# A hybrid convolution, sparse-attention and feed-forward block on one core: merged rows kept in PSUM, x loaded first, woven products and count turns moved

## The reference

```
h  = rmsnorm(x); u = h @ w_in               # [conv a,gate 1024 | q 512 | k,v 64+64 | index q 512 | index k 64 | w 8 | gates 2048]
yc = silu(layernorm(causal_depthwise_conv31(a * sigmoid(gate)))) @ w_conv_out
score[t,s] = sum_heads w[t] * relu(qi[t] . ki[s]),  s <= t;   keep the 256 best keys s of each row t
ya = softmax(q.k/8 - slope*(t-s) over the kept keys) @ v, 8 heads;   ya @ w_attn_out
x1 = x + (sigmoid(gA) * yc + sigmoid(gB) * ya) @ w_out
x2 = x1 + (silu(rmsnorm(x1) @ w_gate) * (rmsnorm(x1) @ w_up)) @ w_down      # inner width 2816
out = rmsnorm(x2)
```

## Time and profile before

| | |
|---|---|
| median of 3 runs | 3352.51 us (3343.8 to 3353.59) |
| the profiled execution | 3356.66 us, span 3354.5 us, mean granted clock 0.981 |
| PE busy | 3200.5 us, 95% of the span |
| DVE, ACT, POOL busy | 2065.4, 1310.3, 743.8 us (62, 39, 22%) |
| chain that ended last | PE 75%, DVE 7%, ACT 4%, issue 4%, DMA 1% |
| DMA | 635.97 MB, mean 190 GB/s |

### The profile page before, as it was taken

The page is one execution under the profiler, slowest core; times in us unless marked ns, Lnnn a source line. Parts: engine busy times, 40 slices in busy tenths (PEclk is TensorE's granted clock), DMA queues, the critical chain, the costliest instruction groups (busy, mean ns, idle before and its releaser), DMA issues.

```text
span 3354.5 us, 41929 instructions
## 1 busy us (share of the span) xinstructions
PE 3200.5 (95%) x15077; PEld 2640.3 (79%) x15077; DVE 2065.4 (62%) x3529; ACT 1310.3 (39%) x2277; POOL 743.8 (22%) x546
## 2 busy tenths in 40 slices
PE   8987999999999999999999999999899998989998
PEld 7865788788888788778887778876788887778886
DVE  5997457688808448598994853759868288610001
ACT  4336421533238431441113843137773177421111
POOL 3431200065774000011322400000211323001212
PEclk9998999999999999999999999999999999999999
DMA  7973756599992656535554055652455510445554
GB/s 228 304 239 122 290 191 207 182 288 291 289 297 108 245 202 218 182 145 195 190 199 145 20 220 203 219 199 81 163 191 198 195 51 20 171 150 193 196 189 169
DMA packets 178528, 635.97 MB, mean 190 GB/s; under 512 B 11357, under 2 KB 96905, under 8 KB 116776
## 3 DMA queue, kind: packets, MB, share of 16 engines
q1 hardware_dynamic: 163728, 582.00, 50.2%
q10 hardware_dynamic: 14616, 51.47, 3.9%
HBM read 474.04 MB, written 159.38 MB: 189 GB/s over the span
## 4 chain that ended last, share of the span: by engine, by line
PE 75%; DVE 7%; ACT 4%; issue 4%; DMA 1%; POOL 0%; ACTq 0%; DVEq 0%; POOLq 0%; SPq 0%
PE PS L1763 19%; PE PS L1725 14%; PE PS L1727 14%; PE PS L1726 14%; PE PS L1930 3%; PE PS L1748 1%; PE PS L1749 1%; PE PS L1750 1%; DVE probs L1593 1%; PE PS L1949 1%; PE PS L1950 1%; PE PS L1809 1%; ACT TMP L838 1%; ACT probs L958 1%; PE PS L1977 1%
## 5 line engine op out<-in xcount | busy, mean ns | idle before, releaser
L1763 PE MATMUL PS<-WS,HT 128*128 128x512 f32 x2088 | 484.3, 392 | 16.1 <-ACT TMP L1082 10.4
L1763 PEld LDWEIGHTS PS<-WS,HT 128*128 128x128 f32 x2088 | 394.5, 189 | 99.7 <-ACT TMP L1082 10.8
L553 POOL TENSOR_TENSOR WS<-RAW,WS 128x1024 fp32r<-128x1024 f32 x116 | 281.1, 2424 | 577.5 <-ACT WS L709 562.2
L1725 PE MATMUL PS<-HF,WS 128*128 128x512 f32 x1024 | 400.5, 391 | 6.9 <-DVE HF L1171 4.6
L637 POOL TENSOR_TENSOR TMP<-TMP 128x512 f32<-128x512 f32 x88 | 113.6, 1291 | 1316.2 <-ACT TMP L1082 1316.2
L1726 PE MATMUL PS<-HF,WS 128*128 128x512 f32 x1024 | 400.1, 391 | 0.0
L1727 PE MATMUL PS<-HF,WS 128*128 128x512 f32 x1024 | 400.0, 391 | 0.0
L1351 DVE TENSOR_SCALAR_CACHE_REDUCE flags<-W,cand 128x640 uint8<-128x640 f32 (+9 forms) x272 | 372.6, 1370 | 35.6 <-DVE cand L1386 27.8
L1725 PE MATMUL PS<-HT,WS 128*128 128x512 f32 x816 | 322.2, 395 | 0.8 <-POOL WS L553 0.6
L1727 PE MATMUL PS<-HT,WS 128*128 128x512 f32 x816 | 317.7, 389 | 0.0
L1726 PE MATMUL PS<-HT,WS 128*128 128x512 f32 x816 | 317.6, 389 | 0.0
(11 more groups left out here) (283 smaller groups left out, 6490.0 us busy)
## 6 DMA issues: line engine op xcount, KB each, us to landing
WS<-split_weights_scratch SPq DMA_DIRECT2D x234, 1024.0 KB, 4.8
split_weights_scratch<-WS SPq DMA_DIRECT2D x116, 1024.0 KB, 5.0
W<-split_weights_scratch SPq DMA_DIRECT2D x114, 1024.0 KB, 4.8
RAW<-in_w_in SPq DMA_DIRECT2D x34, 512.0 KB, 6.0
RAW<-in_w_ffn_gate SPq DMA_DIRECT2D x22, 512.0 KB, 6.3
RAW<-in_w_ffn_up SPq DMA_DIRECT2D x22, 512.0 KB, 6.4
RAW<-in_w_ffn_down SPq DMA_DIRECT2D x22, 512.0 KB, 5.7
gate_b_scratch<-TMP ACTq DMA_DIRECT2D x32, 256.0 KB, 5.3
```

The costliest lines, as they stand in the source:

```text
L553: nc.gpsimd.tensor_tensor(out=WS[:, slot, 1, :], in0=RAW[:, slot, :], in1=WS[:, slot, 0, :].bitcast(f32), op=ALU.subtract).then_inc(w_lo, 1)
L1725: mm(PS[:, bank, :], wh, src[:, 0, k, :], start=k == 0, stop=False)
L1763: ins = mm(PS[:, 2 * t + half, :], lhs, split(c, w_part)[:, half * 512:(half + 1) * 512], start=first and part == 0 and w_part == 0, stop= ...
```

## The change

Nine edits, in the order of the program:

1. **Start.** SP loads all four row tiles of x before anything else (ACT loaded tiles 2 and 3 behind the small vectors). The transposes of the small vectors (`vectors()`, formerly L1772 and L1774, which wait for the seven small loads) move from PE's first place to behind 12 of the 16 scaled-identity products.
2. **Half chunks.** The first half of a half chunk raises a semaphore of its own, `first_half_psum`; DVE's product with the gate waits for that half (L1529 in A, L1639 in C) and no longer for the whole chunk.
3. **Merge in PSUM.** Product and sum of the merge are written in place in banks 0 to 7; ACT and DVE read them there. PE's half chunks no longer wait for `mg_sum`; w_out's first row chunk goes over row tiles 0 to 3 in order, each waiting for the eighths that free its two banks.
4. **POOL in C0.** `lo(c0 + 1)` waits for `at_ready`, so it starts after DVE's low parts of the attention output.
5. **Woven steps.** The 48 matmuls are spread anew: 6 at unit 4, 10 in the last unit, the other 32 evenly between. (Before: evenly over units 4 to last.)
6. **F2.** ACT's count turn behind the gate copy of pair j is done only for j % 4 = 3 (before: for every j not divisible by 4). The turn behind the up copy stays.
7. **C3.** The last two row chunks of w_out are joined row tile by row tile (`last_row_chunks`): each tile's twelve matmuls of both chunks stand together.
8. **C3.** ACT leaves out its waits for PE's chunk counts beside w_out in the last group, which stood ahead of the sum of squares (L731).
9. **F3.** The first gate chunk goes to bank 0 (`pair_bank`) and waits for `t_ready` eighth by eighth, not for all eight.

The diff, its core:

```diff
@@ -123,2 +123 @@
-late = 4
-return range(2 * 3 * KD * max(0, n - late) // (IDX_UNITS[g] - late), 2 * 3 * KD * max(0, n + 1 - late) // (IDX_UNITS[g] - late))
+total, early, late, skip = 2 * 3 * KD, 6, 10, 4
@@ -126 +125 @@
-def pair_bank(p, j):
+    def upto(m):
@@ -128 +127,13 @@
-    return 4 if p == 0 and j % 2 == 0 else 6
+        if m <= skip:
+            return 0
+        if m == IDX_UNITS[g]:
+            return total
+        return early + (total - early - late) * (m - skip - 1) // (IDX_UNITS[g] - skip - 2)
+    return range(upto(n), upto(n + 1))
+def pair_bank(g, p, j):
+    if p == 0 and j % 2 == 0:
+        return 0 if g + 1 == GROUPS and j == 0 else 4
+    return 6
@@ -478 +490 @@
-for t in range(2):
+for t in range(RT):
@@ -625,0 +638 @@
+pool.wait_ge(at_ready, HEADS // 2)
@@ -721,2 +733,0 @@
-for t in range(2, RT):
-    act.dma_start(XA[:, t, :], x_v[:, t, :]).then_inc(x_rows[t], 16)
@@ -1014 +1025 @@
-nc.scalar.activation(HT[:, 0, d, :], GB[:, d, :], ACT.Copy).then_inc(mg_hi, 1)
+nc.scalar.activation(HT[:, 0, d, :], PS[:, d, :], ACT.Copy).then_inc(mg_hi, 1)
@@ -1017,2 +1028,3 @@
-used(c)
-hi(c + 2, c % 2)
+if g + 1 < GROUPS:
+    used(c)
+    hi(c + 2, c % 2)
@@ -1075 +1087 @@
-nc.scalar.activation(TMP[:, s, :], PS[:, pair_bank(p, j), :], ACT.Silu).then_inc(sg_done, 1)
+nc.scalar.activation(TMP[:, s, :], PS[:, pair_bank(g, p, j), :], ACT.Silu).then_inc(sg_done, 1)
@@ -1078 +1090 @@
-if j % 4:
+if j % 4 == 3:
@@ -1082 +1094 @@
-nc.scalar.activation(TMP[:, 2 + s, :], PS[:, pair_bank(p, j) + 1, :], ACT.Copy).then_inc(up_done, 1)
+nc.scalar.activation(TMP[:, 2 + s, :], PS[:, pair_bank(g, p, j) + 1, :], ACT.Copy).then_inc(up_done, 1)
@@ -1526 +1538,4 @@
-dve.wait_ge(w_used, c0 + A_CO + d // 2 + 1)
+if d % 2:
+    dve.wait_ge(w_used, c0 + A_CO + d // 2 + 1)
+else:
+    dve.wait_ge(first_half_psum, 2 * KC * g + d // 2 + 1)
@@ -1636,0 +1652,6 @@
+def merged_lo(d):
+    dve.wait_ge(mg_hi, KD * g + d + 1)
+    nc.vector.tensor_tensor(out=HT[:, 1, d, :], in0=PS[:, d, :], in1=HT[:, 0, d, :].bitcast(f32),
+                            op=ALU.subtract).then_inc(mg_ready, 1)
@@ -1638,3 +1659,6 @@
-dve.wait_ge(w_used, c0 + d // 2 + 1)
-chained(nc.vector.tensor_tensor(out=GB[:, d, :], in0=PS[:, d % 4, :], in1=GB[:, d, :], op=ALU.mult))
-nc.vector.tensor_tensor(out=GB[:, d, :], in0=GB[:, d, :], in1=MA[:, d, :], op=ALU.add).then_inc(mg_sum, 1)
+if d % 2:
+    dve.wait_ge(w_used, c0 + d // 2 + 1)
+else:
+    dve.wait_ge(first_half_psum, KC * (2 * g + 1) + d // 2 + 1)
+chained(nc.vector.tensor_tensor(out=PS[:, d, :], in0=PS[:, d, :], in1=GB[:, d, :], op=ALU.mult))
+nc.vector.tensor_tensor(out=PS[:, d, :], in0=PS[:, d, :], in1=MA[:, d, :], op=ALU.add).then_inc(mg_sum, 1)
@@ -1642,6 +1666,2 @@
-        dve.wait_ge(mg_hi, KD * g + d)
-        nc.vector.tensor_tensor(out=HT[:, 1, d - 1, :], in0=GB[:, d - 1, :], in1=HT[:, 0, d - 1, :].bitcast(f32),
-                                op=ALU.subtract).then_inc(mg_ready, 1)
-dve.wait_ge(mg_hi, KD * (g + 1))
-nc.vector.tensor_tensor(out=HT[:, 1, KD - 1, :], in0=GB[:, KD - 1, :], in1=HT[:, 0, KD - 1, :].bitcast(f32),
-                        op=ALU.subtract).then_inc(mg_ready, 1)
+        merged_lo(d - 1)
+merged_lo(KD - 1)
@@ -1694,0 +1715,8 @@
+def vectors():
+    pe.wait_ge(consts_in, 16 * 7)
+    nc.tensor.transpose(PS[:, 0, 0:44], vrow[:, :], ident[0:44, 0:44])
+    for c in range(KC):
+        ins = nc.tensor.transpose(PS[:, 1, 32 * c:32 * c + TAPS], cwrow[:, c * P:(c + 1) * P], ident[0:TAPS, 0:TAPS])
+    ins.then_inc(vec_psum, 1)
@@ -1699,0 +1728 @@
+vectors()
@@ -1751 +1780,26 @@
-    ins.then_inc(w_used, 1)
+        ins.then_inc(w_used if e else first_half_psum, 1)
+def last_row_chunks(c, src, k, row_done):
+    arrived(c)
+    for t in range(RT):
+        for a in range(2):
+            if t == 0 and a == 1:
+                row_of(c, src, k, 1, False, False)
+                arrived(c + 1)
+            if t != 1 or a == 1:
+                ins = row_of(c + a, src, k + a, t, False, a == 1)
+            if t == RT - 1:
+                ins.then_inc(w_used, 1)
+        if t < RT - 1:
+            ins.then_inc(row_done, 1)
+def row_of(c, src, k, t, first, last):
+    for part in range(2):
+        lhs = src[:, part, k, t * P:(t + 1) * P]
+        for w_part in range(2 - part):
+            for half in range(2):
+                ins = mm(PS[:, 2 * t + half, :], lhs, split(c, w_part)[:, half * 512:(half + 1) * 512],
+                         start=first and part == 0 and w_part == 0, stop=last and part == 1)
+    return ins
@@ -1759,6 +1813 @@
-for part in range(2):
-    lhs = src[:, part, k, t * P:(t + 1) * P]
-    for w_part in range(2 - part):
-        for half in range(2):
-            ins = mm(PS[:, 2 * t + half, :], lhs, split(c, w_part)[:, half * 512:(half + 1) * 512],
-                     start=first and part == 0 and w_part == 0, stop=last and part == 1)
+ins = row_of(c, src, k, t, first, last)
@@ -1771,5 +1819,0 @@
-pe.wait_ge(consts_in, 16 * 7)
-nc.tensor.transpose(PS[:, 0, 0:44], vrow[:, :], ident[0:44, 0:44])
-for c in range(KC):
-    ins = nc.tensor.transpose(PS[:, 1, 32 * c:32 * c + TAPS], cwrow[:, c * P:(c + 1) * P], ident[0:TAPS, 0:TAPS])
-ins.then_inc(vec_psum, 1)
@@ -1819 +1863 @@
-chunk_step(first + i // (3 * KD), pair_bank(0, 0) + i // (3 * KD), HF, i % (3 * KD))
+chunk_step(first + i // (3 * KD), pair_bank(g - 1, 0, 0) + i // (3 * KD), HF, i % (3 * KD))
@@ -1986,3 +2030 @@
-if q >= 2:
-    pe.wait_ge(mg_sum, KD * g + 2 * q - 2)
-half_chunk(c0 + q, [(2 * q) % 4, (2 * q + 1) % 4], lambda part, k: ATS[:, part, k, :],
+half_chunk(c0 + q, [2 * q, 2 * q + 1], lambda part, k: ATS[:, part, k, :],
@@ -1990 +2032 @@
-for k in range(KD):
+for k in range(KD if g + 1 < GROUPS else KD - 2):
@@ -1993,3 +2035,2 @@
-row_chunk(c0 + KC + k, HT, k, k == 0, k == KD - 1, [2, 3, 0, 1] if k == 0 else range(RT),
-          wo_psum if k == KD - 1 else None,
-          {0: (mg_sum, KD * (g + 1) - 2), 1: (mg_sum, KD * (g + 1))} if k == 0 else None)
+row_chunk(c0 + KC + k, HT, k, k == 0, k == KD - 1, range(RT), wo_psum if k == KD - 1 else None,
+          {t: (mg_ready, KD * g + 2 * t + 2) for t in range(RT)} if k == 0 else None)
@@ -1996,0 +2038,2 @@
+pe.wait_ge(mg_ready, KD * (g + 1))
+last_row_chunks(c0 + KC + KD - 2, HT, KD - 2, wo_psum)
@@ -2000,2 +2042,0 @@
-if g == GROUPS - 1:
-    pe.wait_ge(t_ready, KD * (norm_f(g) + 1))
@@ -2004 +2045 @@
-bank = pair_bank(p, j)
+bank = pair_bank(g, p, j)
@@ -2013 +2054 @@
-col_chunk(c0 + 2 * j, bank, HF)
+col_chunk(c0 + 2 * j, bank, HF, t_ready if bank == 0 else None, KD * norm_f(g))
```

More of the change, by code:

```diff
@@ L293, in build_block @@
         at_hi, at_ready = sem("at_hi"), sem("at_ready")
+        first_half_psum = sem("first_half_of_chunk_in_psum")
         gm_in, mg_sum, mg_hi, mg_ready = sem("gates_in"), sem("merged_sum"), sem("merged_hi"), sem("merged_ready")
```

## The result

The kernel after took 3319.7 us (median of 4 runs, 3317.62 to 3320.55) against 3349.32 (4 runs, 3343.8 to 3353.59): ratio 0.9913, 95% interval 0.9901 to 0.9925, 29.6 us faster. The prediction was 3324, range 3310 to 3343; it took its 28.6 us off a median of 3352.51, and a fourth run has since brought before's median to 3349.32. Stage sizes are therefore read from both.

What follows compares the result with a forecast made beforehand. PE, busy 95% of the span, was taken to bound the kernel through its matmuls, waits and lower clock; 1.2 + 2.5 + 1.5 + 4.0 + 2.7 + 1.7 + 6.2 + 8.8 = 28.6 us off 3356.7 gave 3328.1, 3324 against the median; range 3310 to 3343.

Steps and rivals of the forecast that it cites:

- Start: Kernel start through A0: first products up to 2.2 us earlier; 1.2 us taken, lower bound 0.5.
- Half chunks: DVE's gate products start after 12 of 24 matmuls: 2.5 us at A0's end, 1.5 together in A1 to A3.
- 0.5 each: A1 to A3: the last gate product before the first scores' sum comes earlier, 0.5 us per stage, bounds 0 and 2.1 together.
- C1 to C3: nothing gained, nothing lost: Merge in C1 to C3: POOL is silent, PE doesn't wait on the merge, so the change there is worth 0.
- Merge in C0: C0: 1.5 us from POOL behind DVE's low part, 2.3 plus 0.2 from merging in PSUM; 4.0 in all, bounds 1.5 and 5.
- The rival of slow operations in PSUM: Merge in C: in-place PSUM operations are slow, DVE falls behind and PE waits; 3357.5 us, chance 0.04.
- Woven steps: Ends of index scores: ten matmuls fill idle time and keep the clock up; A1 2.7, A2 1.7, A3 1.7 us.
- A1's 1.0 from idle time: A1's end: of PE's 2.2 us idle some comes off beside the clock gain; 1.0 us taken, bounds 0 and 2.2.
- F2: F2: 14.6 us lost are regained, but late marks delay C3's first scores by 8.4; 6.2 remain, bounds 0.9 and 14.6.
- waiting for the first mask by more than 9 us: Sign that the prediction is wrong: C3's scores wait this long for DVE's first mask after F2.
- C3 to F3: Hand-over from C3's last matmuls to F3's first chunk: 10.5 us at full clock less 1.7 clock loss, 8.8 taken.
- sums, squares and identity of tiles 0 and 1 are ready before 2960.7: C3's end: joined row chunks finish tiles 0 and 1 early, so PE waits only for tile 3's sum, until 2962.1.

Runs made afterwards that it cites:

- e12: The kernel after with the start as before (ACT loads row tiles 2 and 3 of x, PE transposes the vectors first): 3320.66 us, one run.
- e10: The kernel after with DVE's products with the gates waiting for the whole half chunk again: 3329.04 us, one run.
- e8: The kernel after without POOL's wait for at_ready ahead of its low part of w_attn_out's second chunk: 3321.66 us, one run.
- e7: The kernel after with the merge's product and sum written to SBUF again: 3323.98 us, ratio to before 0.9926.
- e9: The kernel after with the 48 woven matmuls spread evenly as before: 3325.57 us, ratio to before 0.9922.
- e1: The kernel before, unchanged, run and traced a second time: 3348.77 us.
- e2: The kernel after with ACT's count turns as before (every pair j not divisible by 4): 3324.38 us, ratio to before 0.9925.
- e5: The kernel after with the last two row chunks of w_out in C3 not joined: 3318.08 us, ratio to before 0.9904.
- e6: The kernel after with F3's first gate chunk in bank 4 and waiting for all eight eighths, as before: 3325.53 us, ratio to before 0.9925.
- e3: The kernel after with one more count turn in part 0 of F2, so the 31st falls in part 1: 3308.5 us, ratio to before 0.9881.

## Why the prediction was right, point by point

Against the mean of before's two traces, and the mean of after and those of its variants that share the stage, the parts are 4.8 (to C0), 8.1, 1.8, 6.1 (to C3's first score), 2.1 (C3's scores) and 9.1 (to the end), 32.0 in all, against 3.7, 7.2, 2.2, 6.7, 0 and 8.8 predicted, 28.6 in all. The medians say 29.6. The parts were mostly right in kind; that the total came within 1 us of the measured gain is in part luck, since F2's hand-over gave less than was said and the start, the half chunks and C3's scores more.

- **Start.** Said 1.2 of 2.2: the chunk came 2.2 earlier, and by e12's single trace 1.2 were left. The wait for POOL's low part, said to hold the first chunk back, is gone: the chunk waits 0.27 for DVE. Where in A0 the rest of the gain was lost is open.
- **Half chunks.** The step is mis-sized as far as e10's single trace goes: 2.5 measured 3.0, and "0.5 each" in A1 to A3 measured 0.5, 2.9 and 3.0 with C's part. "C1 to C3: nothing gained, nothing lost" leaned on the early half without saying so: without it each C waits 0.7.
- **Merge in C0.** Right in both places: 1.5 from POOL's wait (e8), 2 to 4 from PSUM (e7). Operations in place took 0.70, not 0.75. The rival of slow operations in PSUM is refuted.
- **Woven steps.** 6.1 said, 3.0 to 5.9 measured (e9). The idle time did fall from 2 to 3 us to 0.9, and the clock stayed up, but a fall of the clock behind 2 to 3 us idle is not certain (1 of 3 failed to come in e1 and in e9), and A1's 1.0 from idle time was not there.
- **F2.** The path was right and the rest mis-sized: 14.3 of the 14.6 lost were won back, and marks took 0.83 per operation of POOL where 0.87 was said. The last link was missing: behind the first sum the queries are loaded before PE can start, so C3's first score came 1.6 us behind the fourth sum. 4.7 (e2) where 6.2 was said. C3's first score came 12.3 us behind F2's end and not 2.3, so the sign "waiting for the first mask by more than 9 us", which the prediction had put under wrong, did show. The reason given for two thirds of POOL's length, "since some of DVE's operations there take one tensor only", doesn't stand: operations with one tensor operand are stretched in after's marks too. The first of these rows began behind a POOL operation (2602.35), the second ahead of the next one (2607.33):

```profile
2602.41 1.51 DVE L1209 TENSOR_SCALAR ties<-W,cand 128x512 f16<-128x512 f32 x1
...
2607.11 0.49 DVE L1209 TENSOR_SCALAR ties<-W,cand 128x512 f16<-128x512 f32 x1
```

  Each POOL operation did not cost its whole length, so the Trainium skill's "the other fully blocks" ("SBUF — State Buffer", section "SBUF: two separate sides") is met by single operations (the 128x2 sum that took 2.40 beside 2.39), while over the marks each POOL operation cost DVE 0.83 us in the mean.
- **C3 to F3.** The sum was right (8.8 said, 9.1 measured) by two errors that cancel. One step was wrong: "sums, squares and identity of tiles 0 and 1 are ready before 2960.7". DVE's program makes that identity behind its sum of tile 3; PE waited 2.80 and not 1.4, and the joining bought nothing (e5). The other: the chunk kept full clock where 1.7 of loss was taken. e6 shows the eighths to be worth 5.8 by the medians. What shortened PE's wait (4.24 to 2.80) is that ACT squares as the sums come, with or without the joining (e5). DVE's sum of tile 3 and the identity behind it, in after:

```profile
2933.66 1.23 DVE L1677 TENSOR_TENSOR XR<-PS,XR 128x1024 f32<-128x1024 f32 x1 [1.49 <-PE PS L1803]
...
2935.99 0.48 DVE L1174 TENSOR_SCALAR YS<-ident,ssq 128x128 f32<-128x128 f32 x2
```

- **C3's scores**, put at nothing, gave 2.1 in the mean, and 4.8 between the two first traces. No edit aimed at this: it is whether a fourth sum falls just behind POOL's operation or just ahead (2.0 us) and how often the clock falls behind the long ones (four times in before's trace, never in after's). Which it is moves with the shifts of the stages ahead (three are long in after, e3, e6, e7, e8, e10, e12, four in e2, e5, e9).

## What to carry to other kernels

Ask of every removed stall which engine is later next and what its tail is worth: 14.3 us came back in F2 and 10.0 went at the next hand-over, because one count turn of 31 fell past a border; one turn moved gave 11.2. Look for small two-input DVE operations beside long ones of GpSimd, since a wait that fixes who goes first cost nothing and gave 9.2. And before crediting an early hand-over, read the order of the consumer's own program.

## What the runs showed of the hardware

- A DVE sum of 128x2 with both inputs in SBUF took 2.36 to 2.42 us when POOL's 2.4 us operation had begun up to 0.05 us ahead, and 0.15 when it began 0.01 to 0.02 us behind, in seven traces; in an eighth (e2) it took 2.42 with POOL 0.01 us behind.
- Operations of DVE with one operand in PSUM were not stretched beside POOL: 32 in place took 0.699 to 0.700 us and 32 low parts 0.680 to 0.693 in after; with both operands in SBUF a low part took up to 2.89 (before) and 2.48 (e7).
- The TensorE clock fell to the lower level (1.2 GHz) behind an idle time of 3.0 us in one execution and stayed at 2.4 GHz behind the same 3.0 us in another of the same program. Behind 2.2 to 2.3 us in C3 it fell four times of four in before's first trace and not once of three in after's; behind 0.9 us at the ends of the index scores it stayed in all three places of after.
